# Token mixers in a new step order, with one inverse-root chain for the next tile and the last

## The chip, the core and the metric

The kernel runs on one core of a Trainium2 chip. The metric is the device time of one execution in microseconds (us). TensorE is called PE here (its weight loads PEld), VectorE DVE, ScalarE ACT, GpSimd POOL and SyncE SP, as in the profile.

## The reference, cut to what matters

One decoder layer over 2048 tokens: an input projection `z`, three token mixers that read it, a merge and output projection, and a routed expert network. The change is in the mixers alone:

```python
sq = rms_norm(sq.reshape(B, S, SWA_Q_HEADS, SWA_HEAD_DIM), swa_q_norm_w[l])
sk = rms_norm(sk.reshape(B, S, SWA_KV_HEADS, SWA_HEAD_DIM), swa_k_norm_w[l])
o_swa = sliding_window_attention(sq, sk, sv, swa_sinks[l])
...
rq = rotary(rq.reshape(B, S, RET_HEADS, RET_QK_DIM))
rk = rotary(rk.reshape(B, S, RET_HEADS, RET_QK_DIM)) * (RET_QK_DIM ** -0.5)
o_ret = head_layer_norm(retention(rq, rk, rv), ret_norm_w[l].reshape(RET_HEADS, RET_V_DIM))
o_ret = jax.nn.silu(rg) * o_ret.reshape(B, S, RET_V_W).astype(x.dtype)
...
mq = rms_norm(mq.reshape(B, S, MEM_HEADS, MEM_HEAD_DIM), mem_q_norm_w[l])
o_mem = memory_attention(mq, mk, mv)
```

So a tile of 128 tokens needs three softmaxes' worth of work (memory heads, and the window heads in two halves), a retention step that carries a state from tile to tile, and inverse square roots for the norms.

## The kernel before

The layer runs in stages with a barrier between them: input norm, input projection, memory keys, the token mixers (`mix_tokens`), mixer projection, output projection and routing, experts. The mixers work on 16 tiles of 128 tokens. Each engine's program is written out by hand: `pipelined` calls `prepare` for the first tile and then `step(a, f, b)`, where `b` is the oldest tile in flight (its outputs are finished here), `f` the next (its scores and probabilities are made here) and `a` the one after that (its norms and rotations are prepared here). An engine takes its instructions strictly in the written order and waits on semaphores.

In a step, PE makes `o_ps` (retention output) and the state products of `b`, turns queries and keys of `f`, makes the memory scores, and then the window scores of `f` in two halves (`window_scores(f, 0)` and `(f, 1)`, lines 965 and 971). All three sets of scores go to one PSUM tensor `scores_ps` in turn, so each must wait until ACT's exponentials have read the set before. DVE takes the row maxima (`window_tops`, lines 858 to 865), ACT the exponentials (`weigh`, line 765). POOL multiplies the probabilities by the inverse sums and makes the four products for the rotations. PE turns the probabilities (`x_probs`), ACT copies them out of PSUM (`take`, line 754) and PE multiplies them with the values (`x_vals`, line 1059). The PSUM regions `F1`, `F2`, `T[0]`, `T[1]` and `O` are used several times in each step; a `Region` counts its fillings and takings.

SP loads a tile's `z` two tiles ahead into one of two buffers: `load` (two parts of `z` and the rotation tables), then `load_values` (the retention values). `store` writes the finished `oT`. All go through one DMA queue in the written order. `inverse_root` is a chain of ten small DVE instructions (lines 502 to 511); it runs twice in a step, on 14 columns for `a` and on 4 for the retention norm of `b`. 

Of the kernel before, what the change touches and what calls it, by code (L numbers as in the profile page):

```python
# [29 lines left out]
P = 128  # L30
# [463 lines left out]
PREPARED = 7  # L494
# [65 lines left out]
def mix_tokens(nc, io, ident, mkT, mv, branch):  # L560
# [14 lines left out]
    with ExitStack() as c:  # L575
# [8 lines left out]
        sq, ss, root, rstd = sb("sq", QK + MW), sb("ss", NH + MEM_H), sb("root", NH + MEM_H), sb("rstd", NH + MEM_H, 2)  # L584
# [5 lines left out]
        mprobs, mprobsT = sb("mprobs", MEM_H * MEM_LEN), sb("mprobsT", MEM_H * MEM_LEN)  # L590
# [10 lines left out]
        st, mva, var, rr, rroot = sb("st", RET_H * 6), sb("mva", RET_H * 2), sb("var", RET_H), sb("rr", RET_H), sb("rroot", RET_H)  # L601
# [12 lines left out]
        def sig(name, per=1, ahead=0):  # L614
# [4 lines left out]
        v_in = [sig(f"v_in{i}", 16) for i in range(2)]  # L619
        o_out = [sig(f"o_out{i}", 16, 1) for i in range(2)]  # L620
# [10 lines left out]
        vals_made = sig("vals_made")  # L631
        stated, aggregated, rscaled, rroot_steps, gated = (
            sig("stated", RET_H), sig("aggregated", RET_H), sig("rscaled"), sig("rroot_steps", 10), sig("gated"))
# [20 lines left out]
        QUARTERS = ((1, 2), (0, 3), (1, 3), (0, 4))  # L654

        @blk.sync
        def _(sp):
# [30 lines left out]
            load(Tile(0, 1))  # L688
            load_values(Tile(0, 1))
# [13 lines left out]
            last = Tile(TILES // 2 - 1, 0)  # L703
            store(last)
# [5 lines left out]
        def _(pool):  # L710
# [14 lines left out]
            def step(a, f, b):  # L725
# [4 lines left out]
                if f:  # L730
                    pool.wait_ge(minverted.sem, minverted.after(f.t))
                    pool.tensor_tensor(heads(mprobs[:], MEM_H), heads(mprobs[:], MEM_H), col(mrinv[:], MEM_LEN),
                                       ALU.mult).then_inc(mprobs_made.sem, 1)
# [8 lines left out]
        def _(act):  # L742
            def prepare(a):
# [6 lines left out]
                act.activation(sq[:, QK:QK + MW], z[:, MQ0:MQ0 + MW], ACT.Square).then_inc(squared.sem, 1)  # L750

# [16 lines left out]
            def step(a, f, b):  # L768
                if b:
                    if not is_tile(b.t, 0):  # L770

                        act.wait_ge(T[1].filled.sem, T[1].filled.after(b.t, 0))
                    act.copy(vals[b.i][:], zt[b.i][:, SV0:SV0 + P]).then_inc(vals_made.sem, 1)
                if f:
                    t = f.t
                    F1.wait_filled(act, t, 0)
                    act.activation(mqT[:], F1.ps[:, 0:MW], ACT.Copy, scale=wm[:, 0:1]).then_inc(F1.taken.sem, 1)
                    F2.wait_filled(act, t, 0)
                    act.activation(kT[f.i][:], F2.ps[:, 0:P], ACT.Copy, scale=wk[:, 0:1]).then_inc(F2.taken.sem, 1)
                    F1.wait_filled(act, t, 1)  # L780
                    act.activation(qT[:], F1.ps[:, 0:4 * P], ACT.Copy, scale=wq[:, 0:1]).then_inc(F1.taken.sem, 1)
                    take(F1, t, 2, rkT[:])
                if b:
                    for n, (region, bt, use) in enumerate(halves(b, 1)):
                        take(region, bt, use, mprobsT[:, n * 512:(n + 1) * 512])
                if f:

                    act.wait_ge(mnegated.sem, mnegated.after(t))
                    for h in range(MEM_H):
                        cols = slice(h * MEM_LEN, (h + 1) * MEM_LEN)  # L790
                        act.activation(mprobs[:, cols], S_ps[:, cols], ACT.Exp, bias=mneg[:, h:h + 1],
                                       scale=rstd[f.i][:, NH + h:NH + h + 1],
# [1625 lines left out]
```

## Time and profile before

| | |
|---|---|
| median of 3 runs | 5087.93 us (5087.92 to 5088.22) |
| profiled execution, its own time | 5087.85 us |
| its span from first to last instruction | 5086.2 us |
| token mixers | from about 1396 to 1914 us of the span |
| granted PE clock, mean over the span | 0.968 |
| DVE's normalised key `x_kn`, once in each tile | 16 times, 1416.0 to 1868.2 us |

The span is measured from the first instruction to the last, and 1.65 us lie around it. The mixers are a tenth of it. Since every tile goes through the same step, the distance from one `x_kn` to the next is the length of a step. In the list of waits, an engine, its line and the engine and line that released it stand in one row; in a timeline, the bracket at the end of a row is the idle time of that engine just before.

### The profile page before, as it was taken

How to read it: one execution, taken by the hardware profiler on the slowest of the kernel's cores; microseconds unless marked ns; L12 is line 12 of the kernel's file. 1: busy time of each engine (PE TensorE's matmuls, PEld its weight loads, DVE VectorE, ACT ScalarE, POOL GpSimd, SP SyncE). 2: the span in 40 equal slices, each digit the busy share in tenths (PEclk: the TensorE clock that was granted, in tenths of full speed). 3: DMA queues.
4: the chain of work that ended last, by engine and by line, in shares of the span. 5: the costliest groups of instructions: out<-in, count | busy, mean ns of one | idle time of the engine just before them, and what ended most of it. 6: DMA issues, size and time to landing. Idle time of an engine off the chain costs nothing. (4 is left out here: it accounts for less than half of the span.)

```text
span 5086.2 us, 98541 instructions
## 1 busy us (share of the span) xinstructions
PE 4789.0 (94%) x31390; PEld 4383.9 (86%) x31391; DVE 2368.9 (47%) x4895; ACT 2047.9 (40%) x3890; POOL 478.0 (9%) x423
## 2 busy tenths in 40 slices
PE   6999999999867778998969999999999999999998
PEld 5888888888656666887869999999999999999997
DVE  4000000000066664335566666676666665665654
ACT  4111111111145553222235555555555555555553
POOL 0000000000033330001210000000101011010100
PEclk7999999999989899999979999999999999999999
DMA  3121212121233333344457776776667576665654
GB/s 121 68 78 66 80 64 82 64 82 56 74 128 123 123 146 145 140 157 153 134 159 219 216 209 204 216 209 205 201 200 210 176 223 193 191 201 180 199 171 110
DMA packets 551243, 759.85 MB, mean 149 GB/s; under 512 B 54496, under 2 KB 455392, under 8 KB 544992
## 3 DMA queue, kind: packets, MB, share of 16 engines
q1 hardware_dynamic: 525328, 671.88, 40.3%
q0 software_dynamic: 25808, 86.59, 7.1%
q8 instruction: 61, 1.00, 0.1%
q14 instruction: 46, 0.38, 0.0%
HBM read 611.45 MB, written 146.87 MB: 149 GB/s over the span
## 5 line engine op out<-in xcount | busy, mean ns | idle before, releaser
L2156 DVE TENSOR_TENSOR e_wlo<-e_raw,e_whi 128x512 fp32r<-128x512 f32 x1552 | 1054.0, 687 | 534.3 <-ACT e_whi L2056 514.6
L2283 PE MATMUL e_acc<-e_xhi,e_whi 128*128 128x272 f32 (+6 forms) x4096 | 1184.3, 289 | 5.1 <-DVEq L2211 2.6
L2285 PE MATMUL e_acc<-e_xlo,e_whi 128*128 128x272 f32 (+6 forms) x4096 | 1179.9, 288 | 0.0
L2284 PE MATMUL e_acc<-e_xhi,e_wlo 128*128 128x272 f32 (+6 forms) x4096 | 1178.3, 288 | 0.0
L2056 ACT CAST e_whi<-e_raw 128x512 fp32r<-128x512 f32 x1552 | 951.8, 647 | 187.2 <-DMA e_raw<-in_w_up 159.1
L2283 PEld LDWEIGHTS e_acc<-e_xhi,e_whi 128*128 128x128 f32 x4096 | 775.0, 189 | 6.2 <-issue 3.0
L2284 PEld LDWEIGHTS e_acc<-e_xhi,e_wlo 128*128 128x128 f32 x4096 | 776.7, 190 | 0.0
L2285 PEld LDWEIGHTS e_acc<-e_xlo,e_whi 128*128 128x128 f32 x4096 | 774.5, 189 | 0.0
L253 PE MATMUL p_acc<-p_hi,hT_hi 128*128 128x512 f32 (+1 forms) x1920 | 734.4, 383 | 15.9 <-DVE p_lo L351 15.9
L254 PE MATMUL p_acc<-p_lo,hT_hi 128*128 128x512 f32 (+1 forms) x1920 | 734.2, 382 | 0.0
L255 PE MATMUL p_acc<-p_hi,hT_lo 128*128 128x512 f32 (+1 forms) x1920 | 734.0, 382 | 0.0
L2283 PE MATMUL e_acc<-e_ahi,e_whi 128*128 128x272 f32 (+6 forms) x2048 | 599.0, 292 | 0.0
L2285 PE MATMUL e_acc<-e_alo,e_whi 128*128 128x272 f32 (+6 forms) x2048 | 588.6, 287 | 0.0
L2284 PE MATMUL e_acc<-e_ahi,e_wlo 128*128 128x272 f32 (+6 forms) x2048 | 587.6, 287 | 0.0
L351 DVE TENSOR_TENSOR p_lo<-p_raw,p_hi 128x512 fp32r<-128x512 f32 (+1 forms) x120 | 78.4, 674 | 1078.6 <-ACT p_hi L322 1078.3
L330 ACT COPY p_z<-p_acc 128x512 f32<-128x512 f32 (+1 forms) x240 | 136.3, 573 | 974.6 <-PE p_acc L255 974.6
L253 PEld LDWEIGHTS p_acc<-p_hi,hT_hi 128*128 128x128 f32 x1920 | 361.5, 188 | 86.2 <-issue 16.3
L255 PEld LDWEIGHTS p_acc<-p_hi,hT_lo 128*128 128x128 f32 x1920 | 361.6, 188 | 70.0
L254 PEld LDWEIGHTS p_acc<-p_lo,hT_hi 128*128 128x128 f32 x1920 | 361.6, 188 | 69.9
L2284 PEld LDWEIGHTS e_acc<-e_ahi,e_wlo 128*128 128x128 f32 x2048 | 387.5, 189 | 0.0
L2283 PEld LDWEIGHTS e_acc<-e_ahi,e_whi 128*128 128x128 f32 x2048 | 386.7, 189 | 0.0
L2285 PEld LDWEIGHTS e_acc<-e_alo,e_whi 128*128 128x128 f32 x2048 | 386.2, 189 | 0.0
(316 smaller groups left out, 5774.5 us busy)
## 6 DMA issues: line engine op xcount, KB each, us to landing
e_raw<-in_w_up SPq DMA_DIRECT2D x1040, 256.0 KB
e_raw<-in_w_down SPq DMA_DIRECT2D x512, 256.0 KB
z<-p_z SPq DMA_DIRECT2D x224, 256.0 KB, 2.0
p_raw<-in_w_in SPq DMA_DIRECT2D x112, 256.0 KB, 3.1
b_gates<-z SPq DMA_DIRECT2D x16, 1536.0 KB
oT<-x_oT SPq DMA_DIRECT2D x16, 1024.0 KB, 4.2
b_raw<-oT SPq DMA_DIRECT2D x16, 1024.0 KB
x_z<-z SPq DMA_DIRECT2D x16, 896.0 KB
```

Of the source, the lines that this page charges most:

```text
L253: pe.matmul(out, x_hi(k), w_hi(k), start=first, stop=False)
L254: pe.matmul(out, x_hi(k), w_lo(k), start=False, stop=False)
L255: mm = pe.matmul(out, x_lo(k), w_hi(k), start=False, stop=last)
L330: act.copy(zs[i % OUTS][:, 0:n], acc[i % BANKS][:, 0:n]).then_inc(copied.sem, 1)
L351: dve.tensor_tensor(w_lo[b][:, k, 0:n], raw[k % RAW][:, 0:n], w_hi[b][:, k, 0:n].bitcast(F32), ALU.subtract).then_inc(lo_made.sem, 1)
L2056: act.copy(held(w_hi, u), loaded(u)).then_inc(hi_made.sem, 1)
L2156: dve.tensor_tensor(held(w_lo, u), loaded(u), held(w_hi, u).bitcast(F32), ALU.subtract).then_inc(lo_made.sem, 1)
L2283: pe.matmul(out, whi, hi[:, k, 0:width], start=k == 0, stop=False)
L2284: pe.matmul(out, wlo, hi[:, k, 0:width], start=False, stop=False)
L2285: mm = pe.matmul(out, whi, lo[:, k, 0:width], start=False, stop=k == KD - 1)
```

## The change

The same work is written in another order on PE, ACT and DVE, and some pieces move to other engines.

- PE turns the memory and window queries and the key of tile `a` at the end of a step instead of the start of the next; the next step begins with the memory scores. The first half of the window scores comes right after the retention outputs, the second where the first stood. A half of the scores is opened as soon as the two exponentials that read that bank are done.
- ACT takes the exponentials of the memory scores first, then the squares of `a`, and no longer copies the window values: SP loads them from `z` in a DMA of their own (`load_window_values`, 128 x 128 values, 64 KB), issued before `store`. ACT copies `x_rqT`, which DVE did.
- DVE makes the inverse sums of the window probabilities at the start of the next step instead of the end of this one, and there is one `inverse_root` chain on 18 columns for `a` and `b` together.
- `x_mprobs` has two buffers. POOL's own order (probabilities of `b`, memory probabilities of `f`, rotations of `a`) stays.

```diff
+            def load_window_values(b):
+                sp.dma_start(vals[b.i][:], z_dram[ds(b.t * P, P), SV0:SV0 + P]).then_inc(vals_in[b.i].sem, 16)
+
...
             with sp.Fori(0, TILES // 2 - 1) as r:
                 for b in (Tile(r, 0), Tile(r, 1)):
 
-                    sp.wait_ge(vals_made.sem, vals_made.after(b.t))
                     sp.wait_ge(gate_made.sem, gate_made.after(b.t))
                     F1.wait_filled(sp, b.t, 1)
                     load(b.plus(2))
 
                     T[1].wait_filled(sp, b.t, 0)
                     load_values(b.plus(2))
+
+                    T[1].wait_filled(sp, b.t, 4)
+                    load_window_values(b.plus(1))
                     store(b)
...
+                    pool.tensor_tensor(heads(mprobs[f.i][:], MEM_H), heads(mprobs[f.i][:], MEM_H),
+                                       col(mrinv[:], MEM_LEN), ALU.mult).then_inc(mprobs_made.sem, 1)
...
+            def take_queries(a):
+                F1.wait_filled(act, a.t, 0)
+                act.activation(mqT[:], F1.ps[:, 0:MW], ACT.Copy, scale=wm[:, 0:1]).then_inc(F1.taken.sem, 1)
+                F1.wait_filled(act, a.t, 1)
+                act.activation(qT[:], F1.ps[:, 0:4 * P], ACT.Copy, scale=wq[:, 0:1]).then_inc(F1.taken.sem, 1)
+                F2.wait_filled(act, a.t, 0)
+                act.activation(kT[a.i][:], F2.ps[:, 0:P], ACT.Copy, scale=wk[:, 0:1]).then_inc(F2.taken.sem, 1)
...
             def step(a, f, b):
-                if b:
-                    if not is_tile(b.t, 0):
-
-                        act.wait_ge(T[1].filled.sem, T[1].filled.after(b.t, 0))
-                    act.copy(vals[b.i][:], zt[b.i][:, SV0:SV0 + P]).then_inc(vals_made.sem, 1)
                 if f:
+                    act.wait_ge(mnegated.sem, mnegated.after(t))
+                    for h in range(MEM_H):
+                        cols = slice(h * MEM_LEN, (h + 1) * MEM_LEN)
+                        act.activation(mprobs[f.i][:, cols], S_ps[:, cols], ACT.Exp, bias=mneg[:, h:h + 1],
+                                       scale=rstd[f.i][:, NH + h:NH + h + 1],
+                                       accum_out=mrsum[:, h:h + 1]).then_inc(mexped.sem, 1)
+                if a:
+                    square(a)
+                if f:
                     take(F1, t, 2, rkT[:])
+                    take(F2, t, 1, rqT[:])
...
-                                       accum_out=mrsum[:, h:h + 1]).then_inc(mexped.sem, 1)
+                    weigh(f, 0)
                 if b:
 
                     act.wait_ge(o_out[b.i].sem, o_out[b.i].after(b.r - 1))
                     take(T[0], b.t, 2, oT[b.i][:, 12 * P:16 * P])
                     probs_turned(b, (0, 1))
                 if f:
-                    weigh(f, 0)
+                    weigh(f, 1)
                 if b:
                     probs_turned(b, (2, 3))
-                if a:
-                    prepare(a)
-                    weigh(f, 1)
...
+                if a:
+                    take_queries(a)
...
+            def invert_roots(a, b):
+
+                if a:
+                    dve.wait_ge(scaled.sem, scaled.after(a.t))
+                if b:
+                    dve.wait_ge(rscaled.sem, rscaled.after(b.t))
+                inverse_root(dve, rstd[(a or b).i], ss, root, rstd_steps, b.t + 2 if b else a.t)
...
             def step(a, f, b):
                 if b:
+                    dve.wait_ge(exped.sem, exped.after(b.t))
+                    dve.wait_ge(sk_exped.sem, sk_exped.after(b.t))
+                    dve.tensor_tensor(rinv[:], rsum[:], sk[:], ALU.add).then_inc(dened.sem, 1)
+                    dve.wait_ge(dened.sem, dened.after(b.t))
+                    dve.reciprocal(rinv[:], rinv[:]).then_inc(inverted.sem, 1)
+                if f:
+                    t = f.t
+                    dve.wait_ge(scored.sem, scored.after(t, 1))
+                    dve.tensor_reduce(mmx[:], heads(S_ps[:], MEM_H), AX, ALU.max).then_inc(mmaxed.sem, 1)
+                    dve.wait_ge(mmaxed.sem, mmaxed.after(t))
+                    dve.scalar_tensor_tensor(out=mneg[:], in0=mmx[:], scalar=-1.0, in1=rstd[f.i][:, NH:RR],
+                                             op0=ALU.mult, op1=ALU.mult).then_inc(mnegated.sem, 1)
                     O.wait_filled(dve, b.t, 0)
+                    for h in range(RET_H):
+                        dve.bn_stats(st[:, 6 * h:6 * h + 6], O.ps[:, h * RET_DV:(h + 1) * RET_DV]).then_inc(stated.sem, 1)
+                if f:
+                    window_tops(f, 0)
+                if b:
+                    dve.wait_ge(stated.sem, stated.after(b.t))
+                    stand(dve, idle)
+                    for h in range(RET_H):
+                        dve.bn_aggr(mva[:, 2 * h:2 * h + 2], st[:, 6 * h:6 * h + 6]).then_inc(aggregated.sem, 1)
                     for h in range(RET_H):
...
+                    dve.wait_ge(aggregated.sem, aggregated.after(b.t))
+                    dve.tensor_scalar(ss[:, RR:RR + RET_H], mva[:].rearrange("p (h a) -> p h a", a=2)[:, :, 1], EPS, None,
+                                      ALU.add).then_inc(rscaled.sem, 1)
+                    dve.wait_ge(mexped.sem, mexped.after(t))
+                    if b:
+                        dve.wait_ge(mprobs_made.sem, mprobs_made.after(b.t))
+                    dve.reciprocal(mrinv[:], mrsum[:]).then_inc(minverted.sem, 1)
+                if a:
+                    sum_squares(a)
                 if f:
...
+                if a or b:
+                    invert_roots(a, b)
+                if a:
+                    normalize_key(a)
+                if f:
+                    window_tops(f, 1)
+                    dve.wait_ge(negated.sem, negated.after(t))
+                    dve.tensor_tensor(sk[:], sinks[:], neg[:], ALU.add).then_inc(sunk.sem, 1)
-                        dve.tensor_scalar(rnorm[:, cols], O.ps[:, cols], mva[:, 2 * h:2 * h + 1], rr[:, h:h + 1],
+                        dve.tensor_scalar(rnorm[:, cols], O.ps[:, cols], mva[:, 2 * h:2 * h + 1],
+                                          rstd[b.i][:, RR + h:RR + h + 1],
                                           ALU.subtract, ALU.mult).then_inc(O.taken.sem, 1)
...
+                if a:
+                    rotate(a)
                 if f:
-                    window_tops(f, 0)
-                if a:
-                    prepare(a)
-                if f:
+                    if b:
+                        dve.wait_ge(gated.sem, gated.after(b.t))
...
-                    dve.wait_ge(exped.sem, exped.after(t))
-                    dve.wait_ge(sk_exped.sem, sk_exped.after(t))
-                    dve.tensor_tensor(rinv[:], rsum[:], sk[:], ALU.add).then_inc(dened.sem, 1)
-                    dve.wait_ge(dened.sem, dened.after(t))
-                    dve.reciprocal(rinv[:], rinv[:]).then_inc(inverted.sem, 1)
...
+            def memory_scores(f):
+
+                F1.wait_taken(pe, f.t, 0)
+                for h in range(MEM_H):
+                    if h % 2 == 0:
+                        pe.wait_ge(exped.sem, exped.after(f.t - 1, SWA_H - 2 + h))
+                    mm = pe.matmul(S_ps[:, h * MEM_LEN:(h + 1) * MEM_LEN], mqT[:, h * P:(h + 1) * P],
+                                   mkT[:, h, :], start=True, stop=True)
+                mm.then_inc(scored.sem, 1)
+
             def window_scores(f, u):
 
                 first = 2 * P if is_tile(f.t, 0) else 0
                 bound = keep[:, first:first + 2 * P].unsqueeze(1).to_broadcast([P, 2, 2 * P])
                 for g in range(SWA_KV):
+                    if u == 0:
+                        pe.wait_ge(mexped.sem, mexped.after(f.t, 2 * (g + 1)))
+                    else:
+                        pe.wait_ge(exped.sem, exped.after(f.t, 2 * (g + 1)))
                     pe.matmul(S_ps[:, g * 512:(g + 1) * 512], turn_keep[:], bound, start=True, stop=False)
                 for j in range(2):
...
+            def prepare(a):
+                z = zt[a.i]
+                pe.wait_ge(z_in[a.i].sem, z_in[a.i].after(a.r))
+                turn(F1, a.t, 0, cuts(z, MQ0 // P, MEM_H))
+                turn(F1, a.t, 1, cuts(z, 0, 4))
+                pe.wait_ge(kn_made.sem, kn_made.after(a.t))
+                turn(F2, a.t, 0, [kn[:]])
+
             def step(a, f, b):
+                if f:
+                    t = f.t
+                    memory_scores(f)
...
+                if f:
+                    F1.wait_taken(pe, t, 1)
+                    F2.wait_taken(pe, t, 0)
+                    window_scores(f, 0)
+                if b:
...
-                    t = f.t
-                    z = zt[f.i]
-                    pe.wait_ge(z_in[f.i].sem, z_in[f.i].after(f.r))
-                    turn(F1, t, 0, cuts(z, MQ0 // P, MEM_H))
-                    pe.wait_ge(kn_made.sem, kn_made.after(t))
-                    turn(F2, t, 0, [kn[:]])
-                    turn(F1, t, 1, cuts(z, 0, 4))
                     pe.wait_ge(rot_made.sem, rot_made.after(t))
+                    turn(F1, t, 2, cuts(rkn[f.i], 0, RET_H))
                     turn(F2, t, 1, cuts(rqn, 0, RET_H))
-
-                    pe.wait_ge(exped.sem, exped.after(t - 1))
-                    F1.wait_taken(pe, t, 0)
-                    for h in range(MEM_H):
-                        mm = pe.matmul(S_ps[:, h * MEM_LEN:(h + 1) * MEM_LEN], mqT[:, h * P:(h + 1) * P],
-                                       mkT[:, h, :], start=True, stop=True)
-                    mm.then_inc(scored.sem, 1)
-                    turn(F1, t, 2, cuts(rkn[f.i], 0, RET_H))
...
                 if f:
-
-                    pe.wait_ge(mexped.sem, mexped.after(t))
-                    window_scores(f, 0)
+                    window_scores(f, 1)
                 if b:
                     turn_probs(b, (2, 3))
-                if f:
-                    pe.wait_ge(exped.sem, exped.after(t, SWA_H // 2))
-                    window_scores(f, 1)
-                if b:
-
+                    pe.wait_ge(vals_in[b.i].sem, vals_in[b.i].after(b.r))
...
+                if a:
+                    prepare(a)
```

PE in a middle step, from the turns of the window probabilities to the next step's retention products. `f_ps` are the regions F1 and F2, `t_ps` T[0] and T[1]. Before:

```order
L965 MATMUL scores_ps<-x_keep,x_turn_keep 128x512 x2
L971 MATMUL scores_ps<-x_kT,x_qT 128x128 x8
L949 MATMUL t_ps<-ident,x_probs 128x128 x4
L528 REGISTER_ALU
L949 MATMUL t_ps<-ident,x_probs 128x128 x4
L1047 ISA
L965 MATMUL scores_ps<-x_keep,x_turn_keep 128x512 x2
L971 MATMUL scores_ps<-x_kT,x_qT 128x128 x8
L534 REGISTER_ALU
L1059 MATMUL t_ps<-x_probsT,x_vals 64x128 x16
L949 MATMUL t_ps<-ident,x_rnorm 128x128 x8
```

The same place of the changed kernel, on to the memory scores:

```order
L1026 MATMUL scores_ps<-x_kT,x_qT 128x128 x8
L990 MATMUL t_ps<-ident,x_probs 128x128 x4
L528 REGISTER_ALU
L990 MATMUL t_ps<-ident,x_probs 128x128 x4
L534 REGISTER_ALU
L1108 MATMUL t_ps<-x_probsT,x_vals 64x128 x16
L990 MATMUL t_ps<-ident,x_rnorm 128x128 x8
L1032 ISA
L528 ISA
L990 MATMUL f_ps<-ident,x_z 128x128 x4
L528 REGISTER_ALU
L990 MATMUL f_ps<-ident,x_z 128x128 x4
```

Only one half of the window scores is left ahead of the values, and the turns of the next tile's `z` follow the turns of `x_rnorm`.

ACT at the start of a middle step. Before:

```order
L773 COPY x_vals<-x_z 128x128
L531 ISA
L777 ACTIVATE x_mqT<-f_ps,x_wm 128x512
L779 ACTIVATE x_kT<-f_ps,x_wk 128x128
L531 REGISTER_ALU
L781 ACTIVATE x_qT<-f_ps,x_wq 128x512
L531 REGISTER_ALU
L754 COPY x_rkT<-f_ps 128x512
```

Of the changed kernel:

```order
L796 ACTIVATE x_mprobs,x_mrsum<-scores_ps,x_mneg,x_rstd 128x256 x4
L755 ISA
L758 ISA
L759 ACTIVATE x_sq<-x_z 128x640
L760 ACTIVATE x_sq<-x_z 128x512
L531 ISA
L776 COPY x_rkT<-f_ps 128x512
L531 REGISTER_ALU
L776 COPY x_rqT<-f_ps 128x512
```

The squares of the tile that is being loaded now stand ahead of the copies that PE waits for.

## Rows read from the trace of the kernel before

**Rows 1.** The page: span and granted clock in 40 slices.

```profile
span 5086.2 us, 98541 instructions
PEclk7999999999989899999979999999999999999999
```

**Rows 2.** Tile `x_kn`: count, duration, first and last start.

```profile
L844 DVE TENSOR_TENSOR x_kn<-x_z,x_rstd x16: 291/292/294, 1416.0 to 1868.2; 128x128 f32<-128x128 f32 x16
```

**Rows 3.** Windows: length; busy PE, PEld, DVE, ACT, POOL; PEclk, DMA share, GB/s.

```profile
1480.00:1840.00 360.00, 277.99 (x2008) 236.25 (x2007) 244.36 (x719) 194.02 (x506) 121.45 (x71) 0.91 0.30 117
```

**Rows 4.** Waits in 1480 to 1840: total us, times, longest.

```profile
PE scores_ps L965 <- ACT x_probs L765: 38.3, 12, 3.2
PE t_ps L949 <- ACT x_oT L754: 36.2, 24, 4.2
...
PE f_ps L949 <- ACT x_mqT L777: 7.4, 11, 0.7
```

**Rows 5.** Timeline of PE, window scores and values of one step.

```profile
1667.42 0.71 PE L965 MATMUL scores_ps<-x_keep,x_turn_keep 128*128 128x512 f32 x2
1668.06 1.16 PE L971 MATMUL scores_ps<-x_kT,x_qT 64*128 64x128 f32 x16
...
1673.44 1.22 PE L965 MATMUL scores_ps<-x_keep,x_turn_keep 128*128 128x512 f32 x2 [3.19 <-ACT x_probs L765]
...
1676.60 3.27 PE L1059 MATMUL t_ps<-x_probsT,x_vals 128*64 128x128 f32 x32
```

**Rows 6.** Timeline of SP, one step's transfers; then two windows (columns as in rows 3).

```profile
1651.24 0.36 SPq L678 DMA_DIRECT2D oT<-x_oT  x1
1652.60 1.51 SPq L669 DMA_DIRECT2D x_z<-z  x2
...
1652.00:1662.00 10.00, 9.33 (x43) 7.77 (x42) 4.33 (x16) 1.64 (x3) 3.60 (x1) 0.83 0.98 375
1662.00:1663.00 1.00, 1.00 (x11) 1.00 (x10) 0.83 (x1) 0.40 (x1) 0.00 (x0) 1.00 0.12 49
```

**Rows 7.** DMA issues of 1500 to 1800: size, median us to landing.

```profile
oT<-x_oT SPq DMA_DIRECT2D x9, 1024.0 KB, 4.2
...
x_z<-z SPq DMA_DIRECT2D x10, 512.0 KB, 6.3
```

**Rows 8.** Timeline of ACT and DVE around one half of the softmax.

```profile
1669.45 1.22 DVE L858 TENSOR_REDUCE x_mx<-scores_ps 128x4 f32<-128x1024 f32 x1
1671.09 0.56 ACT L765 ACTIVATE x_probs<-scores_ps,x_neg,x_rstd 128x256 f32<-128x256 f32 x1 [2.80 <-DVE x_neg L865]
...
1673.18 0.20 ACT L765 ACTIVATION_READ_ACCUMULATOR x_probs<-scores_ps,x_neg,x_rstd 128x1 f32 x1
1673.28 1.07 ACT L754 COPY x_probsT<-t_ps 128x512 f32<-128x512 f32 x2
1674.22 0.77 ACT L749 ACTIVATE x_sq<-x_z 128x640 f32<-128x640 f32 x1
1674.86 0.65 ACT L750 ACTIVATE x_sq<-x_z 128x512 f32<-128x512 f32 x1
```

**Rows 9.** Lines by form, 1480 to 1840: busy us, mean ns | idle before.

```profile
L1059 PE MATMUL t_ps<-x_probsT,x_vals 128*64 128x128 f32 x384 | 35.1, 356 | 0.0
L888 DVE COPY x_rqT<-f_ps 128x512 f32<-128x512 f32 x11 | 7.2, 658 | 0.0
L508 DVE SCALAR_TENSOR_TENSOR x_rroot<-x_rroot,x_var 128x4 f32<-128x4 f32 x33 | 5.4, 162 | 1.1
L732 POOL TENSOR_TENSOR x_mprobs<-x_mprobs,x_mrinv 128x1024 f32<-128x1024 f32 x12 | 22.7, 1894 | 156.6 <-DVE x_mrinv L915 156.6
```

**Rows 10.** Timeline of PE near the end of the mixers, at full clock.

```profile
1868.63 0.60 PE L984 MATMUL o_ps<-x_z,x_inT 128*128 128x256 f32 x2
...
1872.09 1.89 PE L994 MATMUL t_ps<-x_z,x_rkn 128*128 128x256 f32 x8
...
1910.25 1.99 PE L1059 MATMUL t_ps<-x_probsT,x_vals 128*64 128x128 f32 x32 [0.72 <-ACT x_probsT L754]
```

More of the change, by code:

```diff
@@ L493 @@
 CONSTS = 8
-PREPARED = 7
+PREPARED = 8
 def inverse_root(dve, out, x, tmp, steps, t):
@@ L583, in mix_tokens @@
         kT, vals = sb("kT", P, 2), sb("vals", P, 2)
-        sq, ss, root, rstd = sb("sq", QK + MW), sb("ss", NH + MEM_H), sb("root", NH + MEM_H), sb("rstd", NH + MEM_H, 2)
+        sq = sb("sq", QK + MW)
+        ss, root, rstd = sb("ss", NH + MEM_H + RET_H), sb("root", NH + MEM_H + RET_H), sb("rstd", NH + MEM_H + RET_H, 2)
         kn = sb("kn", QK - SK0)
@@ L619, in mix_tokens @@
         v_in = [sig(f"v_in{i}", 16) for i in range(2)]
+        vals_in = [sig(f"vals_in{i}", 16) for i in range(2)]
         o_out = [sig(f"o_out{i}", 16, 1) for i in range(2)]
@@ L703, in _ @@
             last = Tile(TILES // 2 - 1, 0)
+            T[1].wait_filled(sp, last.t, 4)
+            load_window_values(last.plus(1))
             store(last)
@@ L835, in prepare, with normalize_key, rotate @@
                                   ALU.add).then_inc(scaled.sem, 1)
-                dve.tensor_scalar(ss[:, NH:NH + MEM_H], ss[:, NH:NH + MEM_H], 1.0 / MEM_D, EPS, ALU.mult,
+                dve.tensor_scalar(ss[:, NH:RR], ss[:, NH:RR], 1.0 / MEM_D, EPS, ALU.mult,
                                   ALU.add).then_inc(scaled.sem, 1)
-                dve.wait_ge(scaled.sem, scaled.after(t))
-                inverse_root(dve, rstd[a.i], ss, root, rstd_steps, t)
+            def normalize_key(a):
+                t, z = a.t, zt[a.i]
                 if not is_tile(t, 0):
-                    F1.wait_filled(dve, t - 1, 2)
+                    F2.wait_filled(dve, t - 1, 0)
                 dve.tensor_tensor(heads(kn[:], SWA_KV), heads(z[:, SK0:QK], SWA_KV),
                                   col(rstd[a.i][:, SWA_H:NH], SWA_D), ALU.mult).then_inc(kn_made.sem, 1)
+            def rotate(a):
+                t = a.t
                 dve.wait_ge(roped.sem, roped.after(t))
+                if not is_tile(t, 0):
+                    F2.wait_filled(dve, t - 1, 1)
                 for out, cs, sn in ((rqn, qc, qs), (rkn[a.i], kc, ks)):
@@ L911, in step @@
                     dve.tensor_tensor(rnorm[:], rnorm[:], gate[:], ALU.mult).then_inc(gated.sem, 1)
+                if a:
+                    rotate(a)
                 if f:
[L913 to L921 removed]
+                    if b:
+                        dve.wait_ge(gated.sem, gated.after(b.t))
                     dve.wait_ge(tanh_made.sem, tanh_made.after(t))
@@ L1018, in step @@
                     for n, (region, bt, use) in enumerate(halves(b, 1)):
-                        turn(region, bt, use, cuts(mprobs, 4 * n, 4))
+                        turn(region, bt, use, cuts(mprobs[b.i], 4 * n, 4))
                 if f:
@@ L1065, in step @@
                         turn(region, bt, use, cuts(rnorm, 4 * n, 4))
+                if a:
+                    prepare(a)
             pe.wait_ge(prepared.sem, PREPARED)
-            pipelined(pe, lambda a: None, step)
+            pipelined(pe, prepare, step)
 def mixer_constants():
```

72 lines of the change are left out of this document (21 added, 51 removed).

## The prediction, made before the changed kernel ran

> **What bounds the kernel now.** I read the page first: a span of 5086.2 us and a PE clock that is full in most slices but not in those of the mixers [rows 1]. The profiled execution took 5087.85 us, 1.65 more than its span; the median of the three runs, 5087.93, lies 0.08 above it, so a sum made against 5087.85 holds for the median too. The change touches the mixers alone. Their step is read from the instruction that each tile has once: 16 keys from 1416.0 to 1868.2, 15 distances, 30.1 us for a step [rows 2].
>
> Next the windows over twelve middle steps. In 360 us PE is busy for 278, DVE for 244, ACT for 194 and POOL for 121, at a mean granted clock of 0.91 [rows 3]. No engine is full, so the step is set by a ring of waits through several engines, and the list of waits says which: PE stands for ACT's exponentials (38.3 us in 12 steps, 3.2 each), for ACT's copies of `x_oT` (36.2, or 3.0 a step) and for `x_mqT` (0.6 a step) [rows 4]. That is 6.8 us of standing in a step. The standing has a second price. After the 3.19 us gap ahead of the second half of the window scores, the same two groups that took 1.8 us (1667.42 to 1669.22) take over 3 us (1673.44 to 1676.60), and the product with the values takes 3.27 us where it takes 1.99 with the clock at its upper level, 2.4 GHz [rows 5, 10]. By these durations the clock fell from 2.4 to 1.2 GHz in the gap; the mean of 0.91 over the twelve steps has the same origin [rows 3].
>
> The cause is the order: both halves of the window softmax stand at the end of the step, one behind the other, and nothing but one turn of probabilities lies between.
>
> **The change part by part.** The second half of the window scores moves to where the first stood, the first half and the memory scores to the start. Where half a softmax stood bare on PE (3.2 us), there are now the retention outputs, the states, the turns and the memory products. This wait goes, nearly whole. The one ahead of the last turns (3.0) does not: PE must still wait for tops, exponentials and copies of the second half before it can multiply with the values. So I did not take 6.8 us off, but looked for the ring that closes the new step, and found it through SP's queue.
>
> `load` for the next tile is issued behind `store`, which waits for ACT's last copies of `x_oT`. ACT's squares of that tile wait for all of it. In the new order they stand ahead of the copies of `x_rkT`, `x_rqT` and `x_mprobsT`, and these ahead of the exponentials of the first half. In the old order they stood late in the step and waited for nothing. The ring, from one `store` to the next:
>
> 1. The transfer. The store was issued at 1651.24, the first bytes moved at 1652.0 (0.8 us later), and the DMA ran full until 1662.1: 375 GB/s for 10 us and 49 for one, 3.80 MB [rows 6]. Of this the retention values (512 KB, 0.52 MB) are not waited for [rows 7]; the rest takes 3.28/3.80 of 10.1 us, 8.7. A store alone lands 4.2 us after its issue [rows 7]; its 1024 KB at 375 GB/s take 2.8, so 1.4 us lie around it, 0.8 ahead and 0.6 behind. Together 0.8 + 8.7 + 0.6 = **10.1**.
> 2. The squares: 1674.22 to 1675.51 [rows 8], **1.3**.
> 3. Four copies of 512 columns, two in 1.07 [rows 8]: **2.1**.
> 4. Four exponentials: 1671.09 to 1673.38 [rows 8], **2.3**.
> 5. One copy of `x_oT` (0.5) frees the bank for PE's turn of probabilities (0.5) ahead of the scores: **1.0**.
> 6. Window scores, second half, at full clock [rows 5]: **1.8**.
> 7. Maxima to bias, 1669.45 to 1671.05 (ACT begins at 1671.09) [rows 8]: **1.6**.
> 8. Four exponentials **2.3**, two copies **1.1** [rows 8].
> 9. The product with the values: 1.99 at full clock, 3.27 low [rows 5, 10], 35.1 us in 12 steps, 2.9, on average now [rows 9]. PE has stood for some 4 us ahead of it, so I take **2.9**.
> 10. Three copies of `x_oT` (1.6) with one turn between (0.3): **1.9**. Then the store.
>
> The sum is 28.4; with the roundings I take 28.5, against 30.1: 1.6 us a step. Times 15 steps this is 24 us. The first and last steps have less to wait for before and after and I put them at nothing.
>
> The rest of the edits. The second root chain goes from DVE: ten instructions of 0.16 us [rows 9], each waiting for the last, about 2.0 us a step. It lies in DVE's own time, which is 68% full; in the ring only item 7 is DVE's. I count nothing; if DVE's part (two reductions of squares, `x_inT`, the chain, the key) delayed item 7, it would cost, but it runs while ACT and PE do items 3 to 6, 7.2 us, and takes about 5. The copy of `x_rqT` moves from DVE (0.66 [rows 9]) to ACT (0.54) and is in item 3: it costs 0.5 a step. The copy of `x_vals` leaves ACT, 0.3 at the step's start, which is off the ring. Its DMA is 64 KB, 0.2 us of moving at the rate above, issued well before the store, with a whole step until its use; nothing, at most 0.4 us of SP. It is queued ahead of `store`, but the store waits for later copies anyhow. POOL's order is unchanged: memory probabilities 1.9 [rows 9] and then the rotations, which need the tile's load; 34% busy, they end before DVE's `rotate`, which now stands behind the retention norm. No cost.
>
> At item 1 a page weighs against the change. The row gives 1.4 us around a store's moving. The Trainium skill's page "DMA: Bandwidth & Descriptors" (how long a DMA takes, its two cost components) states a fixed part of about 2.0 us, most of it after the last byte; this would make item 1 about 10.7 and the gain by that item 9 us smaller. The row is 0.6 below the page, and the row is used.
>
> **The rivals.**
> - *The transfer lands later than counted, but not fatally.* Completion of the three loads after their last byte is not visible in any row; if it takes 1.2 us instead of the store's 0.6, and the first bytes start 0.4 later because SP issues four transfers, the ring is 29.5 and the gain 0.6 a step: 5079. The page cited above points this way. Chance 0.14.
> - *The ring is PE's.* If the transfer is early, PE's order closes the step: from the store, a copy of queries 0.6, a turn 0.5, memory scores 1.9 (as long as the states, the same shape), retention outputs 3.46 (1868.63 to 1872.09), window scores 1.8, states 1.9 [rows 10], a turn 0.5: 10.7 against 11.4 for items 1 and 2. So the gain grows by at most 0.7 a step, to 5053; if the clock also stays full before the values (0.9 less), to 5040. Against it: a gap of 4 us remains, and gaps of 3 us have dropped the clock. Chance 0.20.
> - *Slower: the load holds up ACT.* ACT's squares stand ahead of the copies that PE waits for. The break-even is an item 1 of 11.7 us. If the load's rows ran at 300 GB/s instead of 375, item 1 would be 12.3, the step 30.7, and PE would have two gaps again, of which the one ahead of the state work drops the clock over the retention outputs (3.5 us more at 1.2 GHz, half of it on the ring): some 32, or +28 us: 5116. For it: SP's queue really is in order. Against it: ten steps moved at 375 steadily. Chance 0.12.
> - *Nothing changes:* the wait removed comes back ahead of the values in full. This needs 1.6 us more somewhere in the ring, such as the low clock over the window scores of item 6 (1.3 more) as well as the values. 5085. Chance 0.08.
>
> **How the numbers follow.** The forecast, 5087.85 - 24 = **5064**, has 0.46 (between 5052 and 5077). Faster and slower are told apart by 0.2%, 10 us, about what a measurement of this kernel can tell from no change. Faster holds the forecast, the PE ring and half of the late transfer: 0.76. Same has the other half, and most of the "nothing" case: 0.13. Slower 0.11. The range: the PE ring with its low end cut at 5044, and above up to 5086, which leaves the slow case and a tip of the low end out, near 2 in 10.
>
> **What the new profile would show.** PE's wait ahead of the second window scores gone; one wait of 4 us ahead of the values, released by ACT's copies of `x_probsT`; ACT waiting some 3 us for the DMA of `x_z` ahead of its squares; a step of 28.5 us between two `x_kn`; clock still near 0.91 in the middle of the mixers. The prediction is wrong if ACT does not wait at the squares, if that wait is over 5 us, or if the gap ahead of the values is gone.

## The result

The changed kernel took 5102.16 us (median of 10 runs, 5100.93 to 5106.96) against 5087.93 for the kernel before beside it (10 runs, 5084.22 to 5090.7): a ratio of 1.003, 95% interval 1.0021 to 1.0038. It is 14 us slower, where the prediction had 24 us faster (5064). The profiled execution took 5101.79 us, its span 5100.1.

The windows, the waits and the key of the changed kernel, over the stretches of [rows 2 to 4]:

```profile
L857 DVE TENSOR_TENSOR x_kn<-x_z,x_rstd x16: 291/293/294, 1415.2 to 1872.0; 128x128 f32<-128x128 f32 x16
...
1480.00:1840.00 360.00, 278.06 (x2007) 231.86 (x2005) 251.57 (x593) 194.59 (x494) 121.43 (x71) 0.90 0.34 124
...
PE t_ps L1108 <- ACT x_probsT L776: 64.5, 11, 6.3
...
ACT x_probs L787 <- DVE x_neg L897: 49.7, 11, 4.9
ACT x_sq L759 <- DMA x_rope<-in_rope: 41.3, 12, 3.9
```

The step went from 30.1 to 30.5 us. TensorE's wait ahead of the second window scores is gone, as it should be. But the one ahead of the values, which was to be 4 us, is 5.9 on average and up to 6.3. ACT waits up to 4.9 us for `x_neg`, VectorE's bias of the second half. VectorE has lost ten instructions and a copy in each step, and is busy for longer, 251.6 us against 244.4 [rows 3].

What it does then is in its timeline, here of one step around the second maxima:

```profile
1644.32 0.67 DVE L847 TENSOR_SCALAR x_ss<-x_ss 128x10 f32<-128x10 f32 x1
...
1644.97 0.67 DVE L944 TENSOR_TENSOR x_inT<-f_ps,x_decayT 128x512 f32<-128x512 f32 x1
1645.57 0.65 DVE L502 TENSOR_SCALAR x_rstd<-x_ss 128x18 int32<-128x18 int32 x1
1646.25 1.20 DVE L506 TENSOR_TENSOR x_root<-x_rstd 128x18 f32<-128x18 f32 x1
1647.49 1.20 DVE L508 SCALAR_TENSOR_TENSOR x_root<-x_root,x_ss 128x18 f32<-128x18 f32 x1
1648.72 1.19 DVE L511 SCALAR_TENSOR_TENSOR x_rstd<-x_root,x_rstd 128x18 f32<-128x18 f32 x1
1649.94 0.18 DVE L506 TENSOR_TENSOR x_root<-x_rstd 128x18 f32<-128x18 f32 x1
...
1651.33 0.29 DVE L857 TENSOR_TENSOR x_kn<-x_z,x_rstd 128x128 f32<-128x128 f32 x1
1651.54 1.22 DVE L890 TENSOR_REDUCE x_mx<-scores_ps 128x4 f32<-128x1024 f32 x1
```

And GpSimd's timeline of the same microseconds:

```profile
1643.06 1.89 POOL L742 TENSOR_TENSOR x_mprobs<-x_mprobs,x_mrinv 128x1024 f32<-128x1024 f32 x1 [11.92 <-DVE x_mrinv L939]
1644.91 1.27 POOL L729 TENSOR_TENSOR x_qc<-x_z,x_rope 128x512 f32<-128x512 f32 x1
1646.14 1.27 POOL L729 TENSOR_TENSOR x_qs<-x_z,x_rope 128x512 f32<-128x512 f32 x1
1647.37 1.28 POOL L729 TENSOR_TENSOR x_kc<-x_z,x_rope 128x512 f32<-128x512 f32 x1
1648.61 1.26 POOL L729 TENSOR_TENSOR x_ks<-x_z,x_rope 128x512 f32<-128x512 f32 x1
```

Read the two together, end by end. `x_qs` ends at 1647.41 and L506 at 1647.45; `x_kc` at 1648.65, L508 at 1648.69; `x_ks` at 1649.87, L511 at 1649.91. An instruction of 0.18 us that starts while a rotation runs ends when the rotation ends. The next rotation has by then begun in the record (`x_kc` at 1647.37, ahead of L508 at 1647.49), and the next link, as an instruction of the chain is called here, ends with that one. The first link after GpSimd is done takes 0.18 again. L847 stands ahead of the rotations and ends at 1644.99, with the memory probabilities `x_mprobs` (1644.95). The maxima in PSUM were ready to be read at about 1649.2 (TensorE's window scores, below) and were read from 1651.54: 2.3 us late. TensorE in the same step:

```profile
1648.05 1.16 PE L1026 MATMUL scores_ps<-x_kT,x_qT 64*128 64x128 f32 x16
...
1656.50 3.73 PE L1108 MATMUL t_ps<-x_probsT,x_vals 128*64 128x128 f32 x32 [6.26 <-ACT x_probsT L776]
```

Over twelve steps (VectorE's groups by form; the chain's three lines stand at 0.52 us, where the same links took 0.16 to 0.17 before [rows 9]):

```profile
L508 DVE SCALAR_TENSOR_TENSOR x_root<-x_root,x_ss 128x18 f32<-128x18 f32 x36 | 18.7, 520 | 1.2
L506 DVE TENSOR_TENSOR x_root<-x_rstd 128x18 f32<-128x18 f32 x36 | 18.6, 517 | 1.2
L511 DVE SCALAR_TENSOR_TENSOR x_rstd<-x_root,x_rstd 128x18 f32<-128x18 f32 x36 | 18.6, 516 | 1.2
L847 DVE TENSOR_SCALAR x_ss<-x_ss 128x10 f32<-128x10 f32 x12 | 8.0, 668 | 0.4
L502 DVE TENSOR_SCALAR x_rstd<-x_ss 128x18 int32<-128x18 int32 x12 | 7.2, 600 | 0.0
```

At 0.175 a link, the thirty-six of each line would be 6.3 us; held, they are 18.6. With L502 and L847 that is 37 + 5 + 6 us in 12 steps, 4.0 us a step. The merged chain saves 2.0, and the two small products behind the maxima, which were held in part of the old steps (means of 0.41 and 0.25 us), are at 0.16 now and give back 0.7.

In the steps of the kernel before, the chains stood at 0.16 to 0.17 us a link. But two signs were there to be read, and I had read neither. The chain of its first tile stood beside the rotations (VectorE, then GpSimd):

```profile
1411.95 1.12 DVE L502 TENSOR_SCALAR x_rstd<-x_ss 128x14 int32<-128x14 int32 x1
1413.10 1.18 DVE L506 TENSOR_TENSOR x_root<-x_rstd 128x14 f32<-128x14 f32 x1
1414.32 0.17 DVE L508 SCALAR_TENSOR_TENSOR x_root<-x_root,x_ss 128x14 f32<-128x14 f32 x1
...
1411.77 1.26 POOL L719 TENSOR_TENSOR x_kc<-x_z,x_rope 128x512 f32<-128x512 f32 x1
1412.99 1.26 POOL L719 TENSOR_TENSOR x_ks<-x_z,x_rope 128x512 f32<-128x512 f32 x1
```

And in ten of the twelve middle steps of the kernel before, the product behind the second maxima (L861, 0.16 us alone) was held too, for up to 1.13 us. Here it ends at 1645.19, one hundredth after the last rotation:

```profile
1644.23 0.96 DVE L861 SCALAR_TENSOR_TENSOR x_mx<-x_mx,x_rstd 128x4 f32<-128x4 f32 x1
...
1643.91 1.27 POOL L719 TENSOR_TENSOR x_ks<-x_z,x_rope 128x512 f32<-128x512 f32 x1
```

### The profile page after: what moved, and what is told of

It is laid out like the page before. It is cut to its first block and busy times, and to the rows that moved or that the text cites. A ratio compares the mean times of both kernels' runs of the same rounds, so it can differ in the third digit from the quotient of the medians.

```text
span 5100.1 us, 98378 instructions
## 1 busy us (share of the span) xinstructions
PE 4791.2 (94%) x31390; PEld 4380.1 (86%) x31391; DVE 2382.1 (47%) x4740; ACT 2053.6 (40%) x3890; POOL 478.1 (9%) x423
```

## The experiments

Theory A: VectorE's small instructions are held by GpSimd's rotations, and this delays the maxima. Theory B: the load of the next inputs, issued behind the store, holds up ACT. Each edit is made to the changed kernel unless said otherwise, and each was timed beside the kernel before, whose median was 5088.44 in the first group, 5088.81 in the second and 5087.63 in the third. "Step" is the distance of the 4th to the 16th `x_kn`, divided by 12: the first three steps are shorter, while the pipeline fills. "End" is TensorE's first product of the stage behind the mixers, 19 us behind the mixers' last store in both kernels; "gap" is TensorE's longest wait right ahead of the values; "link" is the mean of the chain's L508.

| kernel | us | step | end | gap | link, ns |
|---|---|---|---|---|---|
| before | 5087.93 | 31.0 | 1933.2 | none | 162, 174 |
| after | 5102.16 | 31.5 | 1949.4 | 6.3 | 520 |
| r1_rotations_after_tops | 5076.03 | 29.5 | 1922.4 | 4.0 | 178 |
| r2_small_rotations | not comparable | 29.2 | 1914.9 | 4.0 | 178 |
| r3_load_ahead_of_store | 5104.81 | 31.5 | 1950.0 | 6.3 | 518 |
| r4_both | 5068.89 | 29.2 | 1917.9 | 4.0 | 178 |
| r5_chain_after_tops | 5070.4 | 29.4 | 1918.6 | 4.0 | 178 |
| r6_chain_after_tops_load_ahead | 5066.11 | 29.2 | 1913.7 | 4.0 | 178 |
| r7_two_chains | 5132.36 | 33.6 | 1977.9 | 8.3 | 511, 174 |
| r8_short_rotations | 5090.87 | 30.6 | 1936.4 | 5.0 | 380 |
| r9_two_chains_after_tops | 5086.53 | 30.7 | 1933.4 | 4.0 | 164, 174 |

**r1_rotations_after_tops** makes GpSimd wait with the rotations until the second bias is made:

```diff
                 if a:
+                    if f:
+                        pool.wait_ge(negated.sem, negated.after(f.t, 2))
                     prepare(a)
```

> The changed kernel, with one wait added: GpSimd begins the next tile's four rotation products only when VectorE has the bias of the second half of the window scores. Theory A (held VectorE): in the changed kernel VectorE's root chain lies beside the rotation products, and small instructions with two SBUF inputs take 0.52 us in the mean instead of 0.17, some 4.0 us a step; the maxima of the second half start 2.3 us after their scores are there. With the wait, those instructions take 0.17 us again, the step shortens by 2.3 us or more from 30.5 us, and the time falls to 5060 to 5075. Theory B (load and ACT's order): the step is set by the wait of ACT's squares for the tile's load, 3.3 us a step; the time stays within 5 us of 5102.

Measured: 5076.03, ratio 0.9973 (0.9961 to 0.9986), 1 us above theory A's range and 26 below the changed kernel, where theory B had it stay. The links are at 178 ns and the gap at 4.0. One wait makes 26 us of difference. L847 (L849 in this run's numbering) is at 0.67 here as well, beside the memory probabilities, which the edit does not move: of the 4.0 us a step it takes away 3.5.

**r2_small_rotations** leaves out most of the rotation: after the first tile the products take 8 columns of 512, so the outputs differ.

> The changed kernel, but the four rotation products of every tile after the first are made on 8 of 512 columns (this leaves out nearly all of the rotation of those tiles), so GpSimd is nearly idle in the place of the root chain and nothing is moved or made to wait. Theory A: as for the run with the added wait, 5060 to 5075, with root chain instructions at 0.17 us. Theory B: within 5 us of 5102.

Its whole time, 5116.72, can't be used: other values send other numbers of tokens to the experts, and their stage is longer (2592.0 to 5047.8 in place of 2627.4 to 5036.8 in the changed kernel). The mixers can be read: step 29.2, end 1914.9, 34.5 us ahead of the changed kernel. The links are at 178 ns and the gap at 4.0, as with late rotations: theory A has it so. Its step is 0.3 us shorter than r1's.

**r3_load_ahead_of_store** issues the next load when its buffer is free, ahead of the last store:

```diff
+            def load_freed(b):
+                sp.wait_ge(gate_made.sem, gate_made.after(b.t))
+                F1.wait_filled(sp, b.t, 1)
+                load(b.plus(2))
+
+            def rest(b, more=True):
+                T[1].wait_filled(sp, b.t, 0)
+                load_values(b.plus(2))
+                if more:
+                    load_freed(b.plus(1))
+                T[1].wait_filled(sp, b.t, 4)
+                load_window_values(b.plus(1))
+                store(b)
...
```

> The changed kernel with SyncE issuing the next tile's load ahead of the store of the finished tile; the rotations as in the changed kernel. Theory A: ACT's wait at the squares (3.3 us a step) goes, but VectorE is busy without a break from the maxima of the first half to the end of the root chain and the second maxima wait for it, so the time stays within 6 us of 5102. Theory B: the step shortens by up to 3 us, the time falls to about 5060.

Measured: 5104.81, ratio 1.0032 (1.0019 to 1.0045). ACT no longer waits for the load, and now waits for TensorE in the same place:

```profile
ACT x_probs L794 <- DVE x_neg L904: 53.5, 11, 4.9
ACT x_rkT L783 <- PE f_ps L997: 34.8, 12, 2.9
```

So the wait for the transfer was in the profile, as forecast, and was worth nothing here. Theory B falls for the changed kernel.

**r4_both** has both edits.

> Both edits: rotations held until the second bias, and the load ahead of the store. Theory A: with VectorE free, the load is the next thing that closes the ring, and PE's own order is 0.7 us a step behind it: 5 to 15 us below the run with the added wait alone. Theory B: as the run with the load ahead alone, about 5060.

Measured: 5068.89, ratio 0.9963 (0.9949 to 0.9977), 7 us below r1, though the runs of the two overlap (5067.47 to 5073.83 against 5069.48 to 5079.27). With the held chain gone, the transfer is the next wait, worth 0.4 us a step. This kernel also shows the holding from the other side. VectorE's gating of 1024 columns (first row) meets a rotation, and the rotation behind it (second row, GpSimd) lasts 2.26 us in place of 1.27:

```profile
1671.11 1.70 DVE L970 TENSOR_TENSOR x_rnorm<-x_rnorm,x_gate 128x1024 f32<-128x1024 f32 x1
...
1671.68 2.26 POOL L736 TENSOR_TENSOR x_kc<-x_z,x_rope 128x512 f32<-128x512 f32 x1
```

The gating takes 1.22 us where nothing holds it. Here it stands until `x_qs` ends at 1671.73, has 1.1 us left, and in these `x_kc`, begun in the record at 1671.68, stands.

**r5_chain_after_tops** leaves GpSimd alone and moves the chain on VectorE:

```diff
+                if f:
+                    window_tops(f, 1)
+                    dve.wait_ge(negated.sem, negated.after(t))
+                    dve.tensor_tensor(sk[:], sinks[:], neg[:], ALU.add).then_inc(sunk.sem, 1)
                 if a or b:
                     invert_roots(a, b)
                 if a:
                     normalize_key(a)
-                if f:
-                    window_tops(f, 1)
-                    dve.wait_ge(negated.sem, negated.after(t))
-                    dve.tensor_tensor(sk[:], sinks[:], neg[:], ALU.add).then_inc(sunk.sem, 1)
```

> The changed kernel with one edit on VectorE alone: the root chain and the scaled key stand behind the second window maxima in place of ahead of them; GpSimd's order is untouched. Theory A (small VectorE instructions beside GpSimd's rotations are held to the end of a rotation, and this delayed the maxima by 2.3 us): the maxima read PSUM and are not held, the chain starts when the rotations are nearly done, its L508 takes about 180 ns and not 520, TensorE's wait ahead of the values falls from 6.3 us to about 4, the step is 28.3 to 28.9 us, and the time is 5066 to 5080 us. Theory C (not the holding, but the amount of VectorE's work around the maxima, or a chain that must be early for the next step's key and memory products): the step stays above 29.8 us and the time is 5092 to 5110.

Measured: 5070.4, ratio 0.9963 (0.9949 to 0.9977). Theory C falls. The maxima start beside the last rotation (until 1667.19) and take 1.23 us as ever, and the chain starts when the rotations are over:

```profile
1666.96 1.23 DVE L890 TENSOR_REDUCE x_mx<-scores_ps 128x4 f32<-128x1024 f32 x1 [4.01 <-PE scores_ps L1026]
...
1668.91 0.18 DVE L506 TENSOR_TENSOR x_root<-x_rstd 128x18 f32<-128x18 f32 x1
```

VectorE now waits 4.0 us for the scores, where it was 2.3 late for them.

**r6_chain_after_tops_load_ahead** adds r3's edit to r5.

> As r5_chain_after_tops, and the load of the next inputs is issued ahead of the store of the last outputs. Theory A with the transfer as the second wait: 5 to 12 us below r5_chain_after_tops, so 5056 to 5073, as it was 7 between r1_rotations_after_tops and r4_both. If the transfer costs nothing once the chain stands late: within 3 us of r5_chain_after_tops.

Measured: 5066.11, ratio 0.9957 (0.9943 to 0.9971): 4 us below r5, between the two answers; the runs of the two touch (5064.82 to 5070.22 against 5068.02 to 5071.7). By its median it is the fastest kernel of this study.

**r7_two_chains** splits the merged chain again, in the changed kernel's place.

> The changed kernel with the merged root chain split again into two chains in the same place: ten instructions on 4 columns for the last tile, then ten on 14 for the next. Theory A: both lie ahead of the second window maxima, the first is held by the rotations as the merged one is now (L508 about 520 ns), the second runs behind them at about 180 ns a link or is held too, so the maxima come 1.8 to 2.5 us later in 15 of the 16 steps: 5129 to 5142 us. If the merge is worth nothing (its time lies beside other work): within 5 us of 5102.

Measured: 5132.36, ratio 1.0083 (1.0069 to 1.0097), 30 us above the changed kernel, 2.1 us a step. The first chain is held (511 ns a link), the second runs free behind it (174 ns):

```profile
L508 DVE SCALAR_TENSOR_TENSOR x_root<-x_root,x_ss 128x4 f32<-128x4 f32 x33 | 16.9, 511 | 1.1
...
L508 DVE SCALAR_TENSOR_TENSOR x_root<-x_root,x_ss 128x14 f32<-128x14 f32 x33 | 5.7, 174 | 1.1
```

**r8_short_rotations** cuts each rotation product into four:

```diff
-                    pool.tensor_tensor(
-                        dst[:].rearrange("p (h a d) -> p h a d", a=2, d=HALF),
...
+                    for h in range(RET_H):
+                        w = 2 * HALF
...
+                        pool.tensor_tensor(
+                            dst[:, h * w:(h + 1) * w].rearrange("p (h a d) -> p h a d", a=2, d=HALF),
```

> The changed kernel with each of GpSimd's four rotation products of 512 columns cut into four of 128 columns (the same work in 16 instructions); nothing else. From 1.27 us for 512 columns and 0.20 us for 8 a piece should take about 0.45. Theory A in its strict form (a small VectorE instruction that starts beside a GpSimd instruction ends when that one ends): no link of the root chain takes 1.2 us any more, nearly all ten take 0.4 to 0.5, the chain as a whole is some 0.5 to 1.0 us shorter than now, and the time is 5086 to 5100. Theory D (the two engines share their way to the memory, and VectorE's instruction is slowed by a factor, however long GpSimd's is): links beside rotations still take about 1.2 us, there are more of them since the rotations last longer in all, the chain is over 8 us and the time is above 5125.

Measured: 5090.87, ratio 1.0006 (0.9997 to 1.0015). GpSimd has more work (146 us in the window of 360, against 121), and the kernel is 11 us faster than the changed one. VectorE's links, and under them the first eight of the sixteen pieces in GpSimd's timeline:

```profile
1487.44 0.38 DVE L506 TENSOR_TENSOR x_root<-x_rstd 128x18 f32<-128x18 f32 x1
1487.86 0.38 DVE L508 SCALAR_TENSOR_TENSOR x_root<-x_root,x_ss 128x18 f32<-128x18 f32 x1
...
1486.49 1.71 POOL L731 TENSOR_TENSOR x_qc<-x_z,x_rope 128x128 f32<-128x128 f32 x4
1488.16 1.70 POOL L731 TENSOR_TENSOR x_qs<-x_z,x_rope 128x128 f32<-128x128 f32 x4
```

A piece starts every 0.42 us, and so does a link. All ten links are now held (L502 for 0.25 us, the nine others for 0.38), and the chain is shorter: from L502 to `x_kn` 4.0 us (1487.15 to 1491.17) in place of 5.8 (1645.57 to 1651.33). That is more than the 0.5 to 1.0 I expected. Theory D, a slowing by a factor, would have left links of 1.2 us; it falls. At both lengths that were run, 1.27 us and 0.46, a held link costs one GpSimd instruction.

**r9_two_chains_after_tops** splits the chain in r5's place.

> r5_chain_after_tops with the merged root chain split again into two (ten instructions on 4 columns, ten on 14), both behind the second window maxima. If the place decides what the merge is worth: the second chain's 2.0 us lie beside the exponentials and the values, and VectorE has idle time behind them, so the time is within 8 us of r5_chain_after_tops, 5068 to 5079. If VectorE's total work decides: 2.0 us times 15 more, as r7_two_chains was above the changed kernel, 5095 to 5105.

Measured: 5086.53, ratio 0.9997 (0.9988 to 1.0006), 16 us above r5: neither answer. The gap ahead of the values stayed at 4.0, so the chain is off that path; but the normed retention behind it came late for its turn on TensorE, a new wait:

```profile
PE t_ps L1110 <- ACT x_probsT L776: 47.8, 12, 4.0
PE t_ps L992 <- DVE x_rnorm L963: 12.6, 12, 1.7
```

There was cover behind the maxima, but for less than the 2.0 us of a chain: of these 1.05 us a step came out as the wait, and the step grew by 1.3.

This run is also the new order without the merge, both chains behind the maxima, and its time is that of the kernel before (ratio 0.9997). So without the merge the new step order gained nothing in any run here; of the 18 us that r5 lies below the kernel before, 16 are gone when the chain is split again.

## Why the prediction was wrong

**The step that failed** is the one on the root chain: "I count nothing; if DVE's part ... delayed item 7, it would cost, but it runs while ACT and PE do items 3 to 6, 7.2 us, and takes about 5." It added durations read where GpSimd stood idle. In the new place GpSimd rotates, and the part takes 8.7 us (1642.89, the first reduction's start, to the maxima at 1651.54), more than the 7.2 that cover it. Where the links are free the 5 us were right: in r5 the two parts of it take 2.8 and 2.4 us. The companion sentence "POOL's order is unchanged ... No cost" is of the same kind: GpSimd's order had not changed, but what VectorE does beside it had. r1, r5 and r8 show the cause, each from another side. The Trainium skill's page "SBUF — State Buffer" (section "Who interferes with whom") states this rule: VectorE and GpSimd share a port pair, one instruction holds it to its end and the other stands, and a VectorE instruction takes part if it has two inputs in SBUF (against a GpSimd instruction that reads SBUF) or is of a kind that can run in a two-port mode, `tensor_scalar` among them. The traces agree: the links with two SBUF inputs are held (1.20 us), so is the `tensor_scalar` of L847 (0.67, beside `x_mprobs`), and the product with one input in PSUM is not (L944, 0.67 beside `x_qc`; 0.68 in r1 with GpSimd idle).

The sum, item by item, for one ring of the new trace. These rows are its corners: SP's two stores, ACT's first instruction of each item; TensorE's scores and values are shown above.

```profile
1630.84 0.35 SPq L683 DMA_DIRECT2D oT<-x_oT  x1
...
1662.39 0.36 SPq L683 DMA_DIRECT2D oT<-x_oT  x1
...
1640.93 0.74 ACT L759 ACTIVATE x_sq<-x_z 128x640 f32<-128x640 f32 x1 [3.16 <-DMA x_rope<-in_rope]
...
1642.10 0.56 ACT L776 COPY x_rkT<-f_ps 128x512 f32<-128x512 f32 x1
...
1644.05 0.57 ACT L787 ACTIVATE x_probs<-scores_ps,x_neg,x_rstd 128x256 f32<-128x256 f32 x1
...
1646.36 0.58 ACT L776 COPY x_oT<-t_ps 128x512 f32<-128x512 f32 x1
...
1653.19 0.56 ACT L787 ACTIVATE x_probs<-scores_ps,x_neg,x_rstd 128x256 f32<-128x256 f32 x1 [4.92 <-DVE x_neg L897]
...
1660.27 1.17 ACT L776 COPY x_oT<-t_ps 128x512 f32<-128x512 f32 x2 [2.77 <-PE t_ps L1108]
```

| item | forecast | measured |
|---|---|---|
| 1 transfer | 10.1 | 10.1 |
| 2 squares, 3 copies, 4 exponentials | 5.7 | 5.4 |
| 5 handover, 6 scores | 2.8 | 2.8 |
| 7 maxima to bias | 1.6 | 4.0 |
| 8 exponentials and copies | 3.4 | 3.3 |
| 9 values | 2.9 | 3.8 |
| 10 last copies | 1.9 | 2.1 |
| sum | 28.4 | 31.5 |

Item 7 runs from the end of the window scores (1648.05 and 1.16, so 1649.21) to ACT's exponential at 1653.19, item 8 to the values at 1656.50. Item 7 is 2.4 of the 3.1 us. Item 9 is the second, and was mis-sized by itself: with the gap back at 4.0 us in r1 the values still take 43.4 us in 12 steps, 3.6 each. I had taken the mean of the old order for the new one, and had read its 3.27 us as "low", which it is in part only. The granted clock over the values tells them apart (windows as in [rows 3], the clock third from the end: the changed kernel, the kernel before, r9):

```profile
1656.50:1660.23 3.73, 3.73 (x33) 3.40 (x34) 2.68 (x7) 1.00 (x2) 0.93 (x1) 0.51 0.00 0
...
1676.60:1679.87 3.27, 3.27 (x35) 3.10 (x34) 3.05 (x6) 1.50 (x5) 1.42 (x2) 0.60 0.00 0
...
1677.10:1680.25 3.15, 3.15 (x32) 2.74 (x32) 2.98 (x10) 1.00 (x2) 0.00 (x0) 0.61 0.00 0
```

At 0.51 the group ran at 1.2 GHz nearly throughout, and takes 3.73 us; at full clock it takes 1.99 [rows 10]. In the old order the window scores stood between the gap and the values and took the first part of the low clock (0.50 from 1673.44 to 1676.60), and it rose again within the values. In the new order the gap lies right ahead of them.

**The yardstick was too short.** I set 28.5 against the mean of 15 distances, 30.1. From the 4th key (1496.59) to the last, the kernel before needs 31.0 a step; the mean is low because the first two distances are 23.7 and 27.2. A ring forecast is one for the steady steps. This error worked against my own result: with both sides steady, the ring as I summed it would have given 2.5 us in each of 12 steps, 30 us, and not 24.

**Both ends were put at nothing.** From the first instruction of the mixers to the first `x_sk` the changed kernel takes 3.3 us longer (38.3 to 41.6; in r5 it is 38.3 again, so this too is the held chain), and from the last `x_sk` to the next stage 5.8 longer (40.4 to 46.2; still 45.3 in r5). The 14 us are: start 1.1 earlier, head +3.3, fifteen steps +8.2, tail +5.8, all later stages 2.3 shorter. Of the tail, 3.5 us come from the place of the mark: `x_sk` now stands ahead of the gap and the values of its own step, and from it to the last tile's retention outputs there are 7.8 us (1903.2 to 1911.0) in place of 4.4 (1892.8 to 1897.2). The other 2.3 lie behind these; in 1.6 of them TensorE runs the memory products at a granted clock of 0.53 (3.65 us) where it had 1.00 (2.02).

**What held.** None of the three signs that I had named for being wrong came: they looked at ACT, the load and the gap, and none at VectorE. The wait ahead of the second scores is gone, ACT waits 3 to 4 us for the load at the squares, the transfer takes 10.1 us, the clock is near 0.91 (0.90). At the transfer the row was right against the 10.7 that I had worked out by the Trainium skill's page "DMA: Bandwidth & Descriptors". But the first ring I found was not the only one: r3 shows that the step closes without the transfer, through TensorE's own order and VectorE's maxima, and r4 and r6 that the transfer's part in the fast versions is 0.2 to 0.4 us a step. So the rival "the ring is PE's" names the ring that is left when chain and transfer are out of the way, at 29.2 us a step (r4, r6) and not at the 27.8 that it was priced at. That r6's 5066 us is near my 5064 is chance: three terms were off (yardstick, values, ends), not all to the same side. In the chances, the parts that I listed for "faster" add up to 0.73, not 0.76; it changes nothing here.

## What to carry to other kernels

When a chain of small instructions moves on VectorE, look up what GpSimd does in the new place, and read the price from an instance of the same line that already stands beside GpSimd; a spread in one line's durations (0.17 and 1.18 us for the first tile's links, 0.16 to 1.13 for L861) is the sign. In a dependent chain each link can cost a whole GpSimd instruction, as here, so put reductions from PSUM beside GpSimd's work and the chain where it rests, or make GpSimd's instructions short. A saving of instructions is worth what its place is worth: the merge of two chains gave 30 us ahead of the maxima (r7) and 16 us behind them (r9).

## What the runs showed of the hardware

The holding follows single instructions: a link of 0.18 us took 1.20 beside rotations of 1.27 us and 0.38 beside pieces of 0.46. More GpSimd work in shorter instructions was faster by 11 us. Reductions that read PSUM were not held (1.23 us beside `x_kc` at 1642.97 in the kernel before, 1.21 beside the pieces at 1491.59 in r8, 1.22 elsewhere). It holds both ways (a rotation of 1.27 us took 2.26 beside VectorE's gating). The values' duration did not follow the length of the gap ahead of them alone: the product with the values took 3.6 us on average behind gaps of up to 6.3 us and 3.6 behind one of 4.0 in r1, but 3.3 behind the same 4.0 in r9 (39.2 us in 12 steps). In the profile it follows the granted clock: in r9 the clock is still 1.00 in the last 2 us of the gap in nine of twelve steps and falls within the values, in r1 it has fallen before they begin in eleven of twelve. What sets that moment no run here shows.
